# A two-layer encoder in fp32 products: the first layer's ramp into attention, reordered and spread over attention's tiles

## The reference

```python
z = h @ w_in
c_q, c_kv, k_r, g_b, g_c, u = jnp.split(z, ...)        # 384, 256, 64, 512, 512, 512 columns
q = (rms_norm(c_q, q_a_g) @ w_uq).reshape(b, n_total, 4, 192)
kv = (rms_norm(c_kv, kv_a_g) @ w_ukv).reshape(b, n_total, 4, 256)
k_nope, v = kv[..., :128], kv[..., 128:]
k = jnp.concatenate([k_nope, k_rope], axis=-1)         # k_rope: k_r, the same for all heads
q, k = rms_norm(q, q_g), rms_norm(k, k_g)
# the last 64 of the 192 numbers of q and of k are rotated by the token's position
attn = softmax(q k^T * 192 ** -0.5) v
```

## Time and profile before

| | |
|---|---|
| median of 3 runs | 2430.07 us (2429.94 to 2430.51) |
| the profiled execution | 2430.68 us, of which the traced span is 2428.9 us |
| TensorE busy (matmul) | 2330.0 us, 96% of the span |
| VectorE, ScalarE, GpSimd busy | 1265.3, 915.3, 1229.5 us |

### The profile page before, as it was taken

One profiled execution on the slowest core, in us unless ns is written; L12 is line 12 of the kernel. 1 busy time (PEld: TensorE's weight loads), 2 busy tenths in 40 slices (PEclk: granted clock), 3 DMA queues, 4 the chain that ended last, 5 costly groups with the idle time before them and its releaser, 6 DMA issues. The chain is left out here.

```text
span 2428.9 us, 37774 instructions
## 1 busy us (share of the span) xinstructions
PE 2330.0 (96%) x14683; PEld 2124.9 (87%) x14683; DVE 1265.3 (52%) x2049; ACT 915.3 (38%) x1927; POOL 1229.5 (51%) x997
## 2 busy tenths in 40 slices
PE   7999979899999999999998998989999999999998
PEld 7998878899899999999997887888878888888886
DVE  5221377537644444444448468864864444444444
ACT  5124556535322222222225346664532222222221
POOL 1343348544655555555543336764455555555551
PEclk9999989999999999999998999999999999999999
DMA  5131100422111111111112100013211111111111
GB/s 200 45 122 44 40 1 1 160 87 79 57 53 53 49 53 49 49 46 42 53 36 79 34 2 1 1 53 92 79 52 52 52 52 52 53 52 53 53 52 74
DMA packets 186209, 137.20 MB, mean 56 GB/s; under 512 B 7217, under 2 KB 175938, under 8 KB 186034
## 3 DMA queue, kind: packets, MB, share of 16 engines
q1 hardware_dynamic: 185904, 134.71, 17.9%
q10 hardware_dynamic: 130, 0.09, 0.0%
HBM read 121.63 MB, written 12.85 MB: 55 GB/s over the span
## 5 line engine op out<-in xcount | busy, mean ns | idle before, releaser
L2247 POOL TENSOR_TENSOR w_lo<-stage,w_hi 128x512 fp32r<-128x512 f32 x384 | 517.1, 1351 | 638.0 <-ACT w_hi L2148 635.7
L2148 ACT ACTIVATE w_hi<-stage 128x512 fp32r<-128x512 f32 x384 | 239.3, 628 | 585.4 <-PE PS L170 582.8
L2456 DVE TENSOR_TENSOR hT<-hT,PS 128x528 f32<-128x528 f32 (+1 forms) x384 | 266.8, 695 | 335.2 <-PE PS L170 333.8
L168 PE MATMUL PS<-x_hi,w_lo 128*128 128x264 f32 (+2 forms) x1152 | 374.4, 325 | 12.9 <-POOL w_lo L2247 6.8
L169 PE MATMUL PS<-x_lo,w_hi 128*128 128x264 f32 (+2 forms) x1152 | 371.9, 323 | 0.0
L170 PE MATMUL PS<-x_hi,w_hi 128*128 128x264 f32 (+2 forms) x1152 | 371.6, 323 | 0.0
L168 PE MATMUL PS<-s_hi,w_lo 128*128 128x264 f32 (+1 forms) x1104 | 353.4, 320 | 3.1 <-DVE s_lo L2410 3.1
L170 PE MATMUL PS<-s_hi,w_hi 128*128 128x264 f32 (+1 forms) x1104 | 353.9, 321 | 0.0
L169 PE MATMUL PS<-s_lo,w_hi 128*128 128x264 f32 (+1 forms) x1104 | 352.7, 320 | 0.0
L168 PE MATMUL PS<-b_hi,w_lo 128*128 128x264 f32 (+1 forms) x864 | 279.4, 323 | 4.3 <-POOL w_lo L2247 4.3
L169 PE MATMUL PS<-b_lo,w_hi 128*128 128x264 f32 (+1 forms) x864 | 278.9, 323 | 0.0
(11 more groups left out here) (318 smaller groups left out, 4906.8 us busy)
## 6 DMA issues: line engine op xcount, KB each, us to landing
stage<-in_ffn_w SPq DMA_DIRECT2D x280, 256.0 KB, 2.8
stage<-in_even_w_out SPq DMA_DIRECT2D x32, 256.0 KB, 2.7
stage<-in_odd_w_out SPq DMA_DIRECT2D x32, 256.0 KB, 2.6
stage<-in_mla_w_in SPq DMA_DIRECT2D x12, 512.0 KB, 6.3
stage<-in_gqa_w_qkv SPq DMA_DIRECT2D x12, 512.0 KB, 3.6
h_spill<-hT SPq DMA_DIRECT2D x8, 528.0 KB, 5.1
hT<-h_spill SPq DMA_DIRECT2D x8, 528.0 KB, 6.7
conv_hi<-s_hi SPq DMA_DIRECT2D x4, 528.0 KB, 2.7
```

What stands on the lines that cost most here:

```text
L168: T.matmul(out, a_lo, b_hi, start=first, stop=False)
L2148: A.activation(ring(w_hi, n), source(n), ACT.Copy).then_inc(rounded, 1)
L2247: G.tensor_tensor(ring(w_lo, n), source(n), ring(w_hi, n).bitcast(F32), ALU.subtract).then_inc(split, 1)
L2456: V.tensor_tensor(o, o, sums(st.slot), ALU.add).then_inc(drained, 1)
```

## The change

It leaves the arithmetic of every result as it is but for one thing: the squares of an up-projection are now summed without the factor of the latent's inverse root, and the sums are multiplied by its square afterwards, which adds one small VectorE product to each `heads_rsqrt` and one to each `latent_rsqrt`. For the rest it moves work:

- GpSimd scales piece 9 before it splits piece 8.
- GpSimd stages the keys of unit 0 before the last `scale_keys` and before the two memsets of the value tails.
- The rotations of query tiles 5 to 9 were at steps 17, 18, 19 of the loop over 20 up-projections, behind it, and in round 1 of attention. Now tile 5 is at step 18 and tiles 6 to 9 are in attention's rounds 2, 4, 6 and 8.
- The inverse roots of the second group's queries were one block in round 5. Now they are four parts, in rounds 3, 5, 7 and 9.
- The value tails were three instructions on each of ScalarE (round 1) and VectorE (round 2). Now they are apart, in rounds 2, 6, 7 (ScalarE) and 3, 7, 8 (VectorE). The values of unit 0 are rounded and split one round later. Both also hold for the second layer, whose tails are one instruction.
- Rotation tables and scratch lie elsewhere, and the load of `conv(3)` waits for the last tail.

```diff
@@ rsqrt
-        def rsqrt(link, v, y, t, negative=False):
+        def guess_rsqrt(link, v, y, t, negative=False):
...
+        def improve_rsqrt(link, v, y, t):
+
+            link(V.tensor_tensor(t, y, y, ALU.mult))
+            link(V.scalar_tensor_tensor(t, t, -0.5, v, ALU.mult, ALU.mult))
+            link(V.scalar_tensor_tensor(y, t, 1.5, y, ALU.add, ALU.mult))
@@ latent_steps: homes of the tables and of the scratch
-            query_tables = rope[:, :].rearrange("p (j w c f) -> p j w c f", j=TILES, w=2, c=2)
+            query_tables = [m.rearrange("p (w c f) -> p w c f", w=2, c=2) for m in
+                            [wide[:, 2 * NT * Q_RANK + P * j:2 * NT * Q_RANK + P * (j + 1)] for j in range(MAIN)] +
+                            [hT[:, NT * 832:NT * 832 + P]]]
-            rope_tmp, keys_tmp = wide[:, 2 * NT * Q_RANK:8 * UNIT], mid[:, 3584:3584 + 1280]
+            rope_tmp, keys_tmp = stage[:, 2560:3072], mid[:, 3584:3584 + 1280]
@@ copy_up
-                    act.wait_ge(rn_ready, e + 1)
                     act.wait_ge(up_done, n + 1)
...
                     act.wait_ge(up_squared, n + 1)
+                    act.wait_ge(rn_ready, e + 1)
@@ gpsimd
                 for n in range(4, 10):
-                    if n in scaled_pieces:
+                    if n == number[("ukv", 0)]:
                         scale_piece(pool, n)
+                    if n == number[("q", 3)]:
+                        scale_piece(pool, number[("ukv", 1)])
                     split_piece(pool, n)
...
-                for i in range(NT):
+                for i in range(NT - 1):
...
-                pool.wait_ge(scaled, NT)
+                pool.wait_ge(scaled, NT - 1)
+                then(0)
                 pool.wait_ge(lat_done, 2 * NT)
-                for i in range(NT):
+                then(1)
+                scale_keys(NT - 1)
+                for i in range(2, NT):
                     then(i)
@@ begin_heads_rsqrt, latent_rsqrt: one more small product each
+                link(V.tensor_tensor(both, both, factors, ALU.mult))
...
+                    link(V.tensor_tensor(rn_squared[e], rn_lat[e], rn_lat[e], ALU.mult))
@@ vector
-                    if n >= NT + 2:
+                    if NT + 2 <= n <= NT + 6:
                         rotate_queries(dve, link, n - NT - 2)
                     if n == NT + 6:
                         heads_rsqrt(dve, link, Q, 0)
+                    if n == NT + 8:
+                        rotate_queries(dve, link, TILES)
                 then(NT - 1)
-                rotate_queries(dve, link, NT - 2)
@@ vector_at
-                if n == 1:
-                    rotate_queries(dve, link, NT - 1)
-                if n == 5:
-                    heads_rsqrt(dve, link, Q, 1)
+                if n in (2, 4, 6, 8):
+                    rotate_queries(dve, link, TILES + n // 2)
+                if n in (3, 5, 7, 9):
+                    heads_rsqrt(dve, link, Q, 1, [n // 2 - 1])
@@ steps
-            steps.clear_after, steps.keys_after, steps.queries_after = 0, 0, 1
+            steps.clear_after, steps.keys_after, steps.queries_after = 1, 0, 2
@@ attention_phase
+            tails_at = (2, 6, 7) if L0 else (2,)
...
                         load_conv(2)
+
+                        sp.wait_ge(tail_split, len(tail_parts))
                         load_conv(3)
...
-                        if n == 1:
+                        if n == 2:
                             split_values(0)
...
-                            if n == 0:
+                            if n == 1:
                                 round_values(0)
-                            if n == 1:
-                                round_tails()
+                            if n in tails_at:
+                                round_tails(tails_at.index(n))
...
-                        if n == 2:
-                            split_tails()
+                        if n - 1 in tails_at:
+                            split_tails(tails_at.index(n - 1))
```

More of the change, by code:

```diff
@@ L699, in program @@
         up_first = [over(f"up_first{part}", [P, UNIT], F32R, "wide", UNIT * part) for part in range(2)]
-        tails0 = [over(f"tails0{s}", [P, 512], F32, ("w_hi", "w_lo")[s], 2624) for s in range(SEQS)]
+        tails0 = [over("tails00", [P, 512], F32, "w_hi", 2624), over("tails01", [P, 512], F32, "x_lo", 7 * TOKENS)]
         def latent_steps(gates):
@@ L847, in copy_up @@
                         j = i * HEADS0 + hd
-                        last = A.activation(heads_to[e][:, i, hd * size:(hd + 1) * size], part, ACT.Square, scale=r,
+                        last = A.activation(heads_to[e][:, i, hd * size:(hd + 1) * size], part, ACT.Square,
                                             accum_out=heads_ssq[e][:, j:j + 1])
@@ L895, in make_tables @@
                     G.tensor_tensor(k_gain[:, 0:NOPE], k_gain[:, 0:NOPE], q_gain[:, 0:NOPE], ALU.mult).then_inc(tables_made, 1)
[L896 to L900, removed]
+                    shape = [P, 2, 2, ROPE // 2]
+                    halves = q_gain[:, NOPE:QK].rearrange("p (w f) -> p w f", w=2).unsqueeze(2).broadcast_to(shape)
+                    pool.wait_ge(gates.spilled, 16 * KC)
+                    for j in range(TILES):
+                        G.tensor_tensor(query_tables[j], tables[:, j].unsqueeze(1).broadcast_to(shape), halves,
+                                        ALU.mult).then_inc(tables_made, 1)
                 def scale_keys(i):
@@ L987, in rotate_queries @@
                 if i == 0:
-                    dve.wait_ge(tables_made, 3)
+                    dve.wait_ge(tables_made, 1 + TILES)
                 dve.wait_ge(up_copied, NT + i + 1)
@@ L995, in rotate_queries, with heads_rsqrt, begin_heads_rsqrt @@
                 V.engine_nop().then_inc(roped, 1)
-            def heads_rsqrt(dve, link, e, s):
+            def heads_rsqrt(dve, link, e, s, parts=range(4)):
                 n = TILES * HEADS0
                 sums = heads_ssq[e][:, s * n:(s + 1) * n]
+                for part in parts:
+                    if part == 0:
+                        begin_heads_rsqrt(dve, link, e, s, n, sums)
+                    else:
+                        improve_rsqrt(link, v_stat[:, 0:n], sums, t_stat[:, 0:n])
+                    if part == 3:
+                        V.engine_nop().then_inc((rn_k_ready, rn_q_ready)[e], 1)
+            def begin_heads_rsqrt(dve, link, e, s, n, sums):
                 dve.wait_ge(up_squared, e * NT + (s + 1) * TILES)
+                both = sums.rearrange("p (i h) -> p i h", i=TILES)
+                factors = rn_squared[e][:, s * TILES:(s + 1) * TILES].unsqueeze(2).broadcast_to([P, TILES, HEADS0])
+                link(V.tensor_tensor(both, both, factors, ALU.mult))
                 if e == KV:
-                    both = sums.rearrange("p (i h) -> p i h", i=TILES)
                     keys = kr_ssq[:, s * TILES:(s + 1) * TILES].unsqueeze(2).broadcast_to([P, TILES, HEADS0])
@@ L1735, in exponentials, with round_tails @@
                                      accum_out=denominators[0:rows, b:b + 1]).then_inc(exped, 1)
-                    def round_tails():
+                    def round_tails(part):
                         act.wait_ge(tail_in, 16 * 6)
-                        for rounded_tails, raw_tails in tail_parts:
-                            last = A.activation(rounded_tails, raw_tails, ACT.Copy)
-                        last.then_inc(tail_rounded, 1)
+                        rounded_tails, raw_tails = tail_parts[part]
+                        A.activation(rounded_tails, raw_tails, ACT.Copy).then_inc(tail_rounded, 1)
                     def begin(n):
@@ L1851, in output @@
                         if MAIN - 1 in chunks:
+                            pe.wait_ge(tail_split, len(tail_parts) if units[u][0] else 1)
                             T.matmul(PS[:, 7, o0:o0 + m], tail_of(u), p_tail[:, q0:q0 + m], start=False,
```

28 lines of the change are left out of this document (12 added, 16 removed).

## The result

The changed kernel takes 2434.2 us (median of 20 runs, 2431.61 to 2441.27 without one that was disturbed) against 2430.88 us before (20 runs, 2429.19 to 2434.5): a ratio of 1.0019, with a 95% interval of 1.0011 to 1.0026, so 2.7 to 6.3 us slower. A second measurement beside the last experiments gave 1.0017 (1.0006 to 1.0027). By the bound of 0.2% this is no change; by the interval it is a small loss. The profiled execution took 2434.11 us, with a span of 2432.3 us.

A forecast was written before the change was run, and what follows sets the result against it. TensorE, busy 96% of the span, was taken to bound the kernel, its long ramp waits being for VectorE's rests. Ramp -5.3, attention +7.5 and clock +0.5 gave +2.7 on 2430.68, said as 2433 us; range 2422 to 2438.

The forecast's parts named there:

- Pieces in another order: First layer's ramp: scaling piece 9 before splitting piece 8 wins 1.1 us of the 4.84 us wait; bounds 0 and 2.
- keys staged earlier: Ramp, at `up(12)`: the 2.91 us wait goes; 2.9 us of waiting and 1.5 of clock won, 4.4 together.
- Squares ahead of their wait: nothing: Ramp's up-projections: taking squares before waiting for the inverse root changes nothing, since the root is ready long before.
- the wait of 2.36 us at 328.14 stays: Ramp's end: tile 5's rotation takes tile 6's place beside the same GpSimd instruction, so TensorE's 2.36 us wait remains.
- Attention's rounds 2 to 9: First layer: moved SBUF-only VectorE work ahead of the rests waits 12 us for GpSimd; attention 7.5 us later.
- The walk: VectorE's list in attention, rounds 2 to 9, added up round by round from 339.7 to 381.9, against 374.40 before.
- The clock behind the waits: Attention: TensorE at 1.2 GHz behind two waits of over 4 us adds 0 to 2 us, taken as 0.5.
- the clock: Rival, attention: TensorE falls to 1.2 GHz at 344, 357 and 370, each costing 1.5 us; 2437; chance 0.22.
- VectorE gets through: Rival, attention: VectorE keeps its place or meets GpSimd idle, most of the 12 us vanish; 2421; chance 0.27.
- Second layer: Values and tail one round later in the second layer cost nothing, between -1.5 and +0.5 us.

The follow-up runs named there:

- squares_scaled: The changed kernel, but squares of an up-projection take the latent's factor again and the products by its square are gone: 2435.52 us, ratio 1.0020.
- short_gpsimd: The changed kernel with GpSimd's staging and value splits behind the normalisations in rounds 2 to 9 cut to a few columns (results wrong): 2425.93 us, ratio 0.9984.
- layer2_only: The kernel before, with only the second layer's values and tails one round later: 2430.53 us against 2430.62, ratio 0.9998.
- spread_alone: The changed kernel with pieces, keys and squares as before, leaving only the spreading of rotations, roots, values and tails: 2443.16 us, ratio 1.0054.
- parts_behind_rests: The changed kernel with the rotation or part of the roots at the end of each round's VectorE list, behind the rests: 2423.45 us, ratio 0.9974.
- ramp_alone: The changed kernel's edits up to attention (pieces, keys, squares), with rotations, inverse roots, values and tails placed as before: 2422.03 us against 2430.64, ratio 0.9970.
- ramp_parts_behind: The kernel with the ramp's part alone, plus round 1's rotation and round 5's block of roots moved behind their rounds' rests: 2421.62 us, ratio 0.9965.
- changed_again: The changed kernel, unaltered, measured once more on the chip of the last two runs: 2432.65 us, ratio 1.0017, profiled span 2430.6.
- behind_layer2_before: The changed kernel with moved parts behind the rests of their round and the second layer's values and tails as before: 2425.15 us, ratio 0.9978.

## Why the prediction came out right, and where it was wrong

The sum, 2433, was close to both medians (2434.2 and 2432.65), and its range held them. Two of its terms were wrong in opposite directions: the ramp gave 5.2 us more than predicted, and attention, with its clock, took 3.2 more (11.2, not 8.0). A ramp that is won and then lost in attention is what I had predicted. That the number fits so well is luck: the two errors happen to oppose each other, and in the profiled execution 3.2 us of clock in the second layer, which stood in no term, make up for what they leave.

**Pieces in another order, and keys staged earlier: right.** The wait of 4.84 us is 3.69, 1.15 less (said: 1.1). `up(12)` has no wait, the instruction of 3.46 us on VectorE is short, and between 262 and 300 us the shift grows by 4.6 us (said: 4.4, of which 1.5 is clock).

**"Squares ahead of their wait: nothing" and "the wait of 2.36 us at 328.14 stays": wrong, and this is the step that failed.** I read the edit of `copy_up` as a moved wait and priced the product that it adds (0.2 lost). It also takes an operand from every square. Groups of ScalarE by form, 290 to 325 us, first of before and then of the changed kernel:

```profile
L848 ACT ACTIVATE wide<-PS,stat 128x192 f32<-128x192 f32 x29 | 11.8, 419 | 10.6 <-PE PS L170 10.6
```
```profile
L858 ACT ACTIVATE wide<-PS 128x192 f32<-128x192 f32 x36 | 11.4, 331 | 10.7 <-PE PS L170 10.7
```

A square takes 331 ns in place of 419, four of them 0.35 us per up-projection. ScalarE rounds the next transposes that much earlier, and the last instruction of tile 5's rotation starts on VectorE just ahead of GpSimd's staging (318.61 and 318.82; 0.28 us) and not just behind it (321.03 and 320.83 in squares_scaled; 1.35 us). So a wait of 1.32 us (at 305.86 before) becomes 0.90 and that of 2.36 becomes 0.88; between 300 us and the start of attention the shift of TensorE's instructions grows by 4.0 us, where I had 0.2 lost. Squares_scaled shows how much of it is the squares: there it grows by 1.5 in the same stretch, with the same waits as before, and behind the wait of 2.36 us its granted clock is 1.00 over 6 us where it was 0.72 before. So 2.5 us are the squares' and 1.5 the clock's. The ramp gave 10.5 us in this execution and not 5.3: 4.0 + 0.2 from here, and the rest from the clock behind the wait of 4.84 us, which I had let be as it was (the window 210 to 230 has 0.91; it was 0.83). That is chance too: squares_scaled, with a wait of 3.48 us there, has 0.83.

**Attention's rounds 2 to 9: the mechanism was right and the sum too small.** Walked as predicted, the eight rounds should take 42.2 us (339.7 to 381.9); they took 45.9 (329.20 to 375.11), against 33.7 before. Round by round, predicted and measured: 4.0 and 4.1, 7.5 and 9.2, 5.9 and 6.2, 4.1 and 4.2, 4.5 and 4.7, 4.0 and 4.2, 7.7 and 7.8, 4.5 and 5.5. The term that was mis-sized is the waiting for GpSimd, 12 us in the sum and 14.4 in the trace (the moved parts take 23.2 us in the eight rounds, of which 8.85 are their plain work), most of all in round 3: 2.5 us predicted, with one instruction of key staging; the staging has two, and 4.5 - 4 x 0.18 = 3.8 us were lost. With 0.3 more at the transposes behind it that is most of round 3's 1.7; round 9 gave 1.0, in a wait of 0.51 us for TensorE and 2.2 us of waiting for GpSimd (said: 1.5), and the six others 0.1 to 0.3 each. The waits at TensorE were said to be 1.5, 4, 3 with less than 1, and 5; they are 1.70, 5.51, 3.38 with 1.80, and 4.66; one of 1.29 in round 9 was not foreseen. The estimate of one instruction per GpSimd instruction, from the earlier trace rows, held. The rule of the Trainium skill that I cited ("SBUF — State Buffer", section "Who interferes with whom") has the sign and the engines right: short_gpsimd agrees with it (the four roots of round 3 take 1.3 us in place of 4.5).

**The clock behind the waits: about as large as I took it, as far as it can be read.** I took 0.5 us. Windows of the changed kernel (columns as in the earlier trace rows):

```profile
330.00:340.00 10.00, 2.79 (x22) 2.33 (x21) 9.61 (x19) 2.68 (x10) 7.02 (x7) 0.80 0.00 1
340.00:350.00 10.00, 6.62 (x46) 6.35 (x45) 8.47 (x15) 4.59 (x11) 4.95 (x6) 0.84 0.00 0
350.00:360.00 10.00, 8.20 (x52) 7.81 (x50) 9.47 (x23) 3.86 (x11) 5.46 (x7) 0.68 0.01 2
```

TensorE is below full clock in all three, and the transposes behind the longest waits take 0.94 us in place of 0.55 (366.91 above). In rounds 3 and 8 VectorE waits until ScalarE has rounded what these transposes give:

```profile
341.16 0.60 DVE L1911 TENSOR_TENSOR w_lo<-PS,w_hi 128x424 fp32r<-128x424 f32 x1 [1.30 <-ACT w_hi L1739]
...
368.62 0.60 DVE L1911 TENSOR_TENSOR w_lo<-PS,w_hi 128x424 fp32r<-128x424 f32 x1 [1.30 <-ACT w_hi L1739]
```

The walk had 1.0 in each, so 0.6 us more stand in the chain; round 9's wait of 0.51 for TensorE may be of the same kind. The rival "the clock" wanted over 2 us there, and that is not seen. The rival "VectorE gets through" was refuted: VectorE did keep its place for four instructions in rounds 2, 6 and 8 (below), but the rotations took 2.3, 2.3 and 3.6 us, where the walk had 2.0, 2.0 and 4.0.

**Second layer: right.** Nothing, by layer2_only: its interval goes from 2.7 us less to 1.5 more.

**What stays open.** The changed kernel's runs scatter more than those of before: 7 of 19 lie between 2436 and 2441.3, none of before above 2434.5. Attention's balance of +0.3 to +0.7 us explains 0.5 of the 2 to 3.3 us by which the median is higher. That its three long waits more often leave TensorE at 1.2 GHz for longer would fit, but is not shown: those longer executions were not profiled. Nor did I settle why spread_alone's five runs all lie 12 us above before, where its first layer ends 9 us later.

## What to carry to other kernels

Where one engine's list feeds another, put what no one waits for behind what is waited for, before thinking about which round it goes to: for the work spread over attention's rounds that alone was worth some 10 us (parts_behind_rests). Behind the rests, block or spread and ramp or attention make hardly a difference. Ahead of the rests they do: there the spread work cost 10 to 12 us (ramp_alone against the changed kernel), while a single block there was as fast as one behind the rests (ramp_parts_behind). Work on VectorE that reads SBUF alone should be laid beside GpSimd's gaps, and beside GpSimd's rows of instructions its price here was up to one GpSimd instruction per instruction, small as these were. And read an edit for what it takes from each instruction (an operand of an activation), not only for what it adds.

## What the runs showed of the hardware

**How much of a wait's price is chance.** Up to 1400 us layer2_only and the kernel before are the same program, with the same waits of 4.84, 2.91 and 2.36 us, and yet their profiled executions differ by 2.3 us at the start of attention. Windows behind the waits at 214 and 295, of before and then of layer2_only (whose second wait ends at 294.12; the 4 us from there have 1.00 too):

```profile
214.00:220.00 6.00, 5.76 (x16) 4.50 (x17) 0.18 (x1) 0.19 (x1) 0.00 (x0) 0.54 0.00 0
295.00:299.00 4.00, 3.95 (x15) 3.96 (x16) 1.85 (x7) 0.00 (x0) 0.00 (x0) 0.62 0.93 359
```
```profile
214.00:220.00 6.00, 5.80 (x21) 4.81 (x22) 0.14 (x1) 1.10 (x7) 0.00 (x0) 0.72 0.01 4
295.00:299.00 4.00, 4.00 (x27) 3.96 (x26) 0.96 (x3) 1.33 (x7) 0.00 (x0) 1.00 1.00 398
```

The granted clock is 0.54 in one and 0.72 in the other, 0.62 and 1.00 (0.50 would be 1.2 GHz throughout). Behind one and the same wait TensorE stays at 1.2 GHz for a time that differs between executions; between these two it was worth 0.9 us at the first wait and 1.4 at the second. The same is seen where the first layer's 0.7 us went, behind the wait of 1.71 us at 465; of before, the changed kernel and changed_again:

```profile
467.00:472.00 5.00, 3.86 (x25) 3.63 (x24) 1.45 (x3) 1.18 (x3) 0.00 (x0) 0.83 0.00 0
```
```profile
467.00:472.00 5.00, 3.67 (x28) 3.42 (x28) 1.81 (x4) 1.18 (x3) 0.43 (x2) 1.00 0.00 0
```
```profile
467.00:472.00 5.00, 3.86 (x18) 3.49 (x18) 1.49 (x4) 1.18 (x3) 0.11 (x1) 0.66 0.00 0
```

The 3.2 us by which the changed kernel's profiled execution falls back behind 1470 are of this kind, in three pieces (+0.85, +1.2, +1.1, behind waits of 1.83, 3.69 and 4.4 us). The same pieces of 1.2 and 1.1 us stand in the profile of behind_layer2_before, whose second layer is as before, and none stands in changed_again. A single profile, or two, cannot price an edit here to better than 2 or 3 us, and my 1.5 us of clock behind the wait at 295 was as much luck as working.

**Instructions that follow each other without a wait can keep VectorE's place.** Round 6 of the changed kernel, VectorE and then GpSimd:

```profile
353.60 0.28 DVE L695 TENSOR_TENSOR stage<-wide 128x128 f32<-128x128 f32 x1
...
354.20 0.28 DVE L698 TENSOR_TENSOR stage<-wide 128x128 f32<-128x128 f32 x1
354.52 1.01 DVE L699 TENSOR_TENSOR wide<-stage 128x128 f32<-128x128 f32 x1
```
```profile
353.15 2.23 POOL L1701 TENSOR_TENSOR rope<-rope,stat 106x512 f32<-106x512 f32 x1 [1.62 <-DVE stat L1941]
```

The first four instructions of the rotation have no wait between them and take 0.28 us each, and it is GpSimd's normalisation, otherwise 1.04 us, that takes 2.23. The fifth, behind a short gap, is held. GpSimd's instruction started at 353.15, while VectorE was in its maximum (352.99 to 353.68), and the rotation followed that without a pause. The same is seen in rounds 2 and 8, and in round 1 before the change. In round 4 GpSimd's normalisation started at 342.75, before the maximum at 342.81, and there it was the rotation that was held (0.83, 1.35, 1.34 us). So in these five cases the one that came first kept its turn: VectorE's row of instructions against GpSimd's next one, or GpSimd's against VectorE's. The order of arrival is not the whole of it. In round 3, maximum and then GpSimd's normalisation start 0.16 us apart, as in rounds 2, 6 and 8:

```profile
333.38 0.69 DVE L1934 TENSOR_REDUCE stat<-PS 106x1 f32<-106x528 f32 x1
```
```profile
333.54 1.04 POOL L1701 TENSOR_TENSOR rope<-rope,stat 106x512 f32<-106x512 f32 x1 [1.53 <-DVE stat L1941]
```

There it is VectorE's next instruction, the first of the roots, that is held (0.94 us, above), and GpSimd's takes its 1.04. It follows the maximum as closely as a rotation does; what differs is the instruction (128x20, and each of the roots waits for the one before). Which of these decides stays open: no run changed one of them alone.
